# First state-space group projected in the recurrence's last two turns, its running sums moved into the next turn, and modulation blocks spread 1,2,2,2,2,2,2,3

## What is computed

```
hx, hc = rms_norm(...) * (1 + scale) + shift                  # 2 x 256 tokens, 2048 wide
rw, z, xbc, dt, gate = split(h @ w_in)                        # one wide projection, cut in five
ya = rwkv7_branch(centred_token_shift(rw), ...)               # recurrence, 32 heads = 16 pairs
xbc = silu(conv5(xbc) + conv_b);  x, B, C = split(xbc)        # state-space branch, 8 groups
dt  = softplus(dt + dt_bias);  log_a = -exp(a_log) * dt       # step sizes, all 64 heads at once
cs  = cumsum(log_a) in each chunk of 128                      # the running sums
y   = (C B^T * exp(cs_t - cs_s)) (x dt) + C h_in exp(cs)      # chunked scan, forward and backward
yb  = group_rmsnorm(y * silu(z))
mod = silu(c) @ w_mod + b_mod                                 # modulation vector, 6 x 2048
mix = (sigmoid(ga) * (ya @ w_a) + sigmoid(gb) * (yb @ w_b)) @ w_o
out = ... PEER experts on the mixed rows ...
```

## Time and profile before

| what | value |
|---|---|
| median of 3 runs | 3922.86 us (3919.76 to 3926.26) |
| profiled execution, its own time | 3924.12 us |
| its span | 3922.4 us |
| mean granted PE clock over the span | 0.982 |
| PE / DVE / POOL / ACT busy | 90% / 48% / 29% / 17% |
| recurrence, turns 15 and 16 | 1303.07 to 1412.20 us |
| state space, turn 0 / turn 1 | 1412.20 to 1470.90 / 1470.90 to 1548.64 us |
| state space, steady turn (turn 6) | 1836.70 to 1908.54 us |
| state space, turn 7 / turn 8 | 1908.54 to 1977.09 / 1977.09 to 2020.29 us |

### The profile page before, as it was taken

How to read it: one execution, slowest core, us unless ns; L and a number is a source line. 1 busy time by engine, 2 the same in 40 slices (tenths; PEclk the granted TensorE clock), 3 DMA queues, 4 the chain that set the end, 5 groups by cost and what they waited for, 6 DMA issues and landing times. The chain is left out here.

```text
span 3922.4 us, 72007 instructions
## 1 busy us (share of the span) xinstructions
PE 3511.0 (90%) x30704; PEld 2121.7 (54%) x30704; DVE 1866.3 (48%) x3195; ACT 681.6 (17%) x1239; POOL 1126.0 (29%) x1734
## 2 busy tenths in 40 slices
PE   6999999999999789999999999989877777777776
PEld 3556666666666546666688888475332323323322
DVE  1334544544544448877830000156465565564644
ACT  2223223223223112122210000011110110100101
POOL 2044344334335201001000000014444444434432
PEclk9999999999999899999999999999999999999999
DMA  9423222222222157676753435359999999999997
GB/s 353 141 68 82 56 70 76 61 72 70 67 72 66 48 181 236 221 254 199 231 189 145 169 132 202 130 236 425 400 427 427 428 428 427 427 427 428 428 427 313
DMA packets 473393, 906.04 MB, mean 231 GB/s; under 512 B 85181, under 2 KB 307090, under 8 KB 403858
## 3 DMA queue, kind: packets, MB, share of 16 engines
q0 software_dynamic: 73728, 536.90, 32.6%
q1 hardware_dynamic: 307664, 318.46, 24.6%
q10 hardware_dynamic: 91714, 46.43, 4.1%
HBM read 889.04 MB, written 12.68 MB: 230 GB/s over the span
## 5 line engine op out<-in xcount | busy, mean ns | idle before, releaser
L2570 PE MATMUL ps<-w_slots,diag 128*128 128x512 f32 x1920 | 887.9, 608 | 267.3 <-DMA w_slots<-in_peer_v,ixv 235.2
L2570 PEld LDWEIGHTS ps<-w_slots,diag 128*128 128x128 f32 x1920 | 351.6, 192 | 801.5 <-issue 449.3
L1006 PE MATMUL ps<-hT,w_slots 128*128 128x512 f32 (+1 forms) x1536 | 617.9, 536 | 4.1 <-PEq L231 2.2
L1696 PE MATMUL ps<-hT,w_slots 128*128 128x256 f32 (+1 forms) x1504 | 496.2, 486 | 6.9 <-PEq L667 4.9
L2183 POOL DMA_INDIRECT w_slots<-in_peer_v,ixv x244 | 264.0, 1082 | 600.3 <-PE ps L2570 498.6
L2347 DVE SCALAR_TENSOR_TENSOR junk<-w_slots,hT 128x2048 f32<-128x2048 f32 x128 | 293.5, 2293 | 269.8 <-DMA w_slots<-in_peer_u,ixu 269.5
L2347 DVE SCALAR_TENSOR_TENSOR junk<-ybT,hT 128x2048 f32<-128x2048 f32 x128 | 293.4, 2292 | 263.9 <-DMA ybT<-in_peer_u,ixu 263.5
L1696 PEld LDWEIGHTS ps<-hT,w_slots 128*128 128x128 f32 x1504 | 283.8, 191 | 179.6 <-issue 158.6
L1006 PEld LDWEIGHTS ps<-hT,w_slots 128*128 128x128 f32 x1536 | 270.7, 189 | 172.4 <-issue 147.8
L736 POOL TENSOR_TENSOR Ypart<-Ym,Sm 128x126 f32<-128x126 f32 (+22 forms) x496 | 185.0, 373 | 488.7 <-DMA Sm<-s_blocks 451.1
L880 DVE SCALAR_TENSOR_TENSOR w_slots<-ps,em,w_slots 128x64 f32<-128x64 f32 x448 | 106.4, 279 | 306.0 <-PE ps L1075 306.0
(11 more groups left out here) (383 smaller groups left out, 4381.2 us busy)
## 6 DMA issues: line engine op xcount, KB each, us to landing
w_slots<-in_w_mod SPq DMA_DIRECT2D x128, 512.0 KB, 5.7
w_slots<-in_w_in SPq DMA_DIRECT2D x56, 1024.0 KB, 6.2
w_slots<-in_w_in ACTq DMA_DIRECT2D x44, 1024.0 KB, 7.9
w_mod_ring<-in_w_mod SPq DMA_DIRECT2D x16, 2048.0 KB, 15.6
w_slots<-in_w_in SPq DMA_DIRECT2D x7, 4096.0 KB, 12.7
w_slots<-in_w_branch_a SPq DMA_DIRECT2D x4, 4096.0 KB, 12.8
w_slots<-in_w_branch_b SPq DMA_DIRECT2D x4, 4096.0 KB, 12.6
w_slots<-in_w_out SPq DMA_DIRECT2D x4, 4096.0 KB, 12.7
```

The costliest lines, as they stand in the source:

```text
L1006: last = mm(ps[:, 4, t0:TOK], w[m % 2][:, k, :], hT[:, k, t0:TOK], start=(k == 0), stop=(k == KC - 1))
L1696: last = mm(out, w[m % SLOTS_W][:, k, :], hT[:, k, t0:TOK], start=(k == 0), stop=(k == KC - 1))
L2570: last = nc.tensor.matmul(ps[:, 4 * n + c, :], diag[:, k % 2, :], vb[k % NB][:, c * 512:(c + 1) * 512], start=False, stop=False)
```

## The change

It has four parts.

- **Projections moved.** Turn 15 of the recurrence now projects x0, x1 and the step sizes (in the places of "k", "r", "v"), turn 16 projects C, z0 and z. Of the first group only B is left for `ssd`. Their weight tiles are loaded by SP as slots fall free: z0 into w[0] when x0 is done, C into w[3] when `solved` has read it, z into w[1], B into w[2] when the last read of the keys is done. A second `Marks` (`ss_early`) counts them. The two outputs of turn 16 follow each other at once, z0 and z stand behind the mean and behind the variance, and the variance lies in the upper half of bank 6 in every turn.
- **First turn of `ssd` in another order.** ACT copies x0, x1, C and takes silu of z0 and z before the exponentials; DVE's convolutions stand between the steps of log_a; the weight tiles 7, 8 and 9 are loaded there, tile 6 (x0 of group 1) behind B.
- **Running sums inside turn 1.** PE makes them after seven k-steps of group 1's x0; `rows`, `crossed` and the transposes of B follow after four k-steps of x1. DVE's copy of the sums, the convolution of B and the whole first modulation block follow each other.
- **Modulation blocks** 1 in turn 0, 2 in turns 1 to 6, 3 in turn 7; `by_row` has a third row, and a plain count takes the place of the marks.

```diff
+                    if i == PAIRS - 1:
+                        sp.wait_ge(*ss_early.by("x0", 0))
+                        sp.dma_start(w[0], w_in[:, :, Z0:Z0 + P]).then_inc(ss_loads[0], 16)
+                        sp.wait_ge(*PB.by("wu3", i))
+                        sp.dma_start(w[3], w_in[:, :, C0:C0 + P]).then_inc(ss_loads[3], 16)
+                        sp.wait_ge(*ss_early.by("x1", 0))
+                        sp.dma_start(w[1], w_in[:, :, Z0 + P:Z0 + 2 * P]).then_inc(ss_loads[1], 16)
+                    if i == PAIRS:
+                        sp.wait_ge(*VB.by("zt1", PAIRS - 1))
+                        sp.dma_start(w[2], w_in[:, :, B0:B0 + P]).then_inc(ss_loads[2], 16)
...
+                EARLY = {"x0": (0, 1, ps[:, 4, :]), "x1": (1, 1, ps[:, 5, :]), "C": (3, 1, ps[:, 1, SEQ:TOK]),
+                         "z0": (0, 2, ps[:, 2, SEQ:TOK]), "z": (1, 2, ps[:, 3, SEQ:TOK])}
...
                         if A:
                             project(name, p, k0, k1)
-                        elif name == "k":
-                            (next_tile if B else step_sizes)(k0, k1)
+                        elif B and name == "v":
+                            step_sizes(k0, k1)
+                        elif B:
+                            early_tile({"k": "x0", "r": "x1"}[name], k0, k1)
+                        else:
+                            early_tile({"k": "C", "r": "z0", "v": "z"}[name], k0, k1)
...
+                    if Z and not B:
+                        outputs(1, z, i)
...
+                    else:
+                        piece("r", 0, 5)
                     if Z:
-                        need(pe, AA, "n1", p)
                         need(pe, AD, "std", z - 1)
                         pe.wait_ge(*AD.by("ysq", z))
-                        mm(ps[:, 7, 0:SEQ], head_mean[:, :], ysq[:, :], start=True, stop=True).then_inc(*PD.did("var"))
+                        mm(ps[:, 6, SEQ:TOK], head_mean[:, :], ysq[:, :], start=True, stop=True).then_inc(*PD.did("var"))
+                    if not A and not B:
+                        piece("r", 5, KC)
+                        piece("v", 0, 6)
...
-        MOD0, MOD_PER = 2 * KC, 4 * KC // GROUPS
+        MOD0 = 2 * KC
+        MOD_BLOCKS = {0: (0,), **{t_: (2 * t_ - 1, 2 * t_) for t_ in range(1, 7)}, 7: (13, 14, 15)}
...
+                padded(0, 0)
+                padded(0, 1)
+                padded(0, 3)
+                for n in range(2):
+                    act.wait_ge(ya_out[n], 8 * PAIRS)
+                gate(0)
                 act.wait_ge(rows_sem, 32)
...
+                padded(0, 2)
+                silu(0, 0)
+                silu(0, 1)
                 act.wait_ge(sums, 1)
...
                     def mods(m0, m1):
-                        for m in range(m0, m1):
+                        blocks = MOD_BLOCKS[i] if A else ()
+                        for m in range(m0 * len(blocks) // 2, m1 * len(blocks) // 2):
...
                     def piece(n, k0, k1):
-                        if A and (n, i) != (0, 0):
+                        if A and (i or n == 2):
                             project(n, i, k0, k1)
...
                     piece(0, 4, 7)
                     if B:
-                        rows(g)
-                        crossed(g)
+                        if g == 0:
+                            running_sums()
+                        if g:
+                            rows(g)
+                            crossed(g)
...
+                    if g == 0:
+                        pe.wait_ge(heads_done, 1)
+                        rows(g)
+                        crossed(g)
+                        pe.wait_ge(*AB_.by("tx0", g))
+                        turned("tB", 2, 2, g)
```

More of the change, by code:

```diff
@@ L1373, in _ @@
                 sp.dma_start(a_exp[:, :], a["ssm_a_log"].rearrange("l d h -> l (d h)").broadcast_to([P, 2 * SH])).then_inc(rows_sem, 16)
-                for n in range(2, SLOTS_W):
-                    tile(sp, n)
                 for n in range(2):
@@ L1427, in _, with padded @@
             def _(act):
+                bank = lambda i, n: (5 * i + n) % 2 if i or n > 1 else 4 + n
+                projected = lambda i, name: early.by(name, 0) if i == 0 and name != "B" else PA.by(name, i)
+                def padded(i, n):
+                    act.wait_ge(*projected(i, TILES[n]))
+                    if i or n > 1:
+                        tile(act, 6 * i + n + SLOTS_W)
+                    past(act, VA, f"c{n}_4", i - 1)
+                    if n < 3:
+                        nc.scalar.activation(pad[:, n, 0, 2:SEQ + 2], ps[:, bank(i, n), 0:SEQ], ACT.Copy)
+                    nc.scalar.activation(pad[:, n, 1, 2:SEQ + 2].rearrange("p (w r) -> p w r", r=GRID_R),
+                                         in_columns(ps[:, bank(i, n), SEQ:TOK]), ACT.Copy).then_inc(*AA.did(f"p{n}"))
@@ new lines, in silu, with gate @@
+                def silu(i, n):
+                    t0 = SEQ if n == 3 else 0
+                    act.wait_ge(*VA.by(f"c{n}_4", i))
+                    nc.scalar.activation(cv[:, i % 2, n, t0:TOK], cv[:, i % 2, n, t0:TOK], ACT.Silu).then_inc(*AA.did(f"s{n}"))
+                def gate(i):
+                    act.wait_ge(*projected(i, "z0"))
+                    tile(act, 6 * i + 4 + SLOTS_W)
+                    act.wait_ge(*projected(i, "z"))
+                    tile(act, 6 * i + 5 + SLOTS_W)
+                    past(act, VB, "out", i - 2)
+                    gate_in = ps[:, bank(i, 4), :].rearrange("p (e t) -> p e t", e=2) if i else ps[:, 2:4, SEQ:TOK]
+                    nc.scalar.activation(sz[:, i % 2, :, :], gate_in, ACT.Silu).then_inc(*AA.did("z"))
```

272 lines of the change are left out of this document (141 added, 131 removed).

## The result

| | before | after |
|---|---|---|
| median (11 runs each, same chip) | 3925.03 us | 3940.05 us |
| ratio after / before | | 1.0039, 95% interval 1.0031 to 1.0047 |
| profiled execution's span | 3922.4 us | 3941.1 us |
| S, the start of the state space | 1412.20 us | 1420.48 us |
| S to `states` 1 of turn 1 | 86.0 us | 80.2 us |

The kernel became slower, by 15 us in the medians (12 to 18 by the interval), where +5.7 was forecast. The median lies 0.05 us above the upper end of the range, 3940.

What follows compares the result with a forecast made beforehand. PE was taken to bound the state space. A longer recurrence (+5.3 us), a shorter way from the block's start to `states` 1 (-9.8) and turn 7 (+10.2) gave +5.7: median 3922.86 to 3928.5 us, range 3914 to 3940.

Runs made afterwards that it cites:

- run 7: The changed kernel with modulation cut into 16, 34, 34, 34, 34, 34, 35, 35 steps in turns 0 to 7; 3932.07 us, 1.0022 of before.
- run 9: The changed kernel with tile 6 loaded in the recurrence, tiles 8, 9 by SP, yaT in turn 2, modulation steps 10, six times 35, 36, earlier sums; 3904.58 us.

## What to carry to other kernels

When work leaves a block that is bound by one engine, first ask what the block's transfers need: add up the bytes asked for between its start and the first load that someone waits for, and divide by the rate of a window in which the DMA engines are near 1.0, not by a single load's time. Load the first tile that the next stage wants into the slot that falls free first, even if the natural numbering gives it another. And hand out filler work in pieces smaller than the idle time it is meant to fill: 16 steps did not fit into 10.5 us, 2 or 3 more a turn cost nothing in turns 2 to 6 of run 7 and, but for the slow k-steps of turn 3, of run 9.
